# First norm of a decoder layer: rounded copies on GpSimd, scaling on ScalarE alone, projections started behind four tiles

## What is computed

```python
def rmsnorm(x, g):
    xf = x.astype(jnp.float32)
    y = xf * lax.rsqrt(jnp.mean(xf * xf, axis=-1, keepdims=True) + EPS)
    return (y * g.astype(jnp.float32)).astype(x.dtype)
...
    h = rmsnorm(x, w['norm1_g'])
    proj = h @ w['w_in']
...
    x = x + merged @ w['w_out']
    h2 = rmsnorm(x, w['norm2_g'])
    up = h2 @ w['ffn_up']
    x = x + (jax.nn.silu(g_ff) * u_ff) @ w['ffn_down']
```

## Time and profile before

| what | value |
|---|---|
| median of 3 runs | 1821.24 us |
| lowest, highest | 1820.85, 1821.57 us |
| the profiled execution, its own time | 1820.36 us |
| its span in the profile | 1818.4 us |
| PE busy | 1759.6 us (97% of the span) |
| DVE busy | 1047.0 us (58%) |
| POOL busy | 771.4 us (42%) |
| ACT busy | 518.5 us (29%) |

### The profile page before, as it was taken

The page is one execution under the profiler, slowest core; times in us unless marked ns, Lnnn a source line. Parts: engine busy times, 40 slices in busy tenths (PEclk is TensorE's granted clock), DMA queues, the critical chain, the costliest instruction groups (busy, mean ns, idle before and its releaser), DMA issues.

```text
span 1818.4 us, 31230 instructions
## 1 busy us (share of the span) xinstructions
PE 1759.6 (97%) x11711; PEld 1695.9 (93%) x11711; DVE 1047.0 (58%) x1459; ACT 518.5 (29%) x730; POOL 771.4 (42%) x622
## 2 busy tenths in 40 slices
PE   6999989999999999999999999899999999999997
PEld 5999877888899989999999999899999999999997
DVE  6774356536543344232253389977677778666666
ACT  6110144423321122011031032544444444200012
POOL 2433210123223343343352234699989895323330
PEclk9999999999999999999999999999999999999999
DMA  5111220032132222322325421322222225422302
GB/s 157 37 45 41 73 68 25 13 88 70 42 90 71 83 80 71 99 62 73 88 64 132 125 83 48 94 71 70 88 75 82 70 70 213 153 95 94 114 0 96
DMA packets 168917, 146.10 MB, mean 80 GB/s; under 512 B 14679, under 2 KB 151772, under 8 KB 168791
## 3 DMA queue, kind: packets, MB, share of 16 engines
q1 hardware_dynamic: 164983, 131.72, 24.2%
q10 hardware_dynamic: 3841, 13.14, 1.9%
HBM read 111.59 MB, written 33.21 MB: 80 GB/s over the span
## 4 chain that ended last, share of the span: by engine, by line
PE 54%; DVE 9%; POOL 6%; issue 2%; ACT 1%; DMA 0%; POOLq 0%; DVEq 0%; SPq 0%; ACTq 0%
PE ps L2678 8%; PE ps L2684 8%; PE ps L2681 8%; PE ps L3159 5%; DVE cv L2481 2%; PE ps L3285 2%; PE ps L3279 2%; PE ps L3282 2%; PE ps L3309 2%; PE pt L3309 2%; PE ps L3311 2%; PE ps L3310 2%; PE pt L3311 2%; PE pt L3310 2%; POOL slot L1326 2%
## 5 line engine op out<-in xcount | busy, mean ns | idle before, releaser
L1175 POOL TENSOR_TENSOR mark<-eps 128x1 f32<-128x1 f32 x123 | 41.3, 336 | 778.5 <-PE ps L2684 283.8
L2678 PE MATMUL ps<-h_hi,w_hi 128*128 128x352 f32 x1608 | 358.7, 331 | 7.1 <-ACT y_all L1524 5.0
L2684 PE MATMUL ps<-h_hi,w_lo 128*128 128x352 f32 x1608 | 346.9, 323 | 0.0
L2681 PE MATMUL ps<-h_lo,w_hi 128*128 128x352 f32 x1608 | 346.2, 323 | 0.0
L2678 PEld LDWEIGHTS ps<-h_hi,w_hi 128*128 128x128 f32 x1608 | 267.5, 189 | 13.2 <-issue 10.7
L2684 PEld LDWEIGHTS ps<-h_hi,w_lo 128*128 128x128 f32 x1608 | 275.5, 188 | 0.0
L2681 PEld LDWEIGHTS ps<-h_lo,w_hi 128*128 128x128 f32 x1608 | 273.4, 188 | 0.0
L1182 POOL TENSOR_TENSOR w_lo<-w_raw,w_hi 128x1024 fp32r<-128x1024 f32 x69 | 181.0, 2623 | 5.5
L2481 DVE SCALAR_TENSOR_TENSOR cv<-ext,pv,cv 128x1072 f32<-128x1072 f32 x88 | 168.3, 1912 | 9.3 <-DVE fstate L2479 2.0
L2602 DVE TENSOR_TENSOR x_acc<-x_acc,ps 128x352 f32<-128x352 f32 (+3 forms) x136 | 70.4, 518 | 43.1 <-PE ps L3311 39.1
L2602 DVE TENSOR_TENSOR x_acc<-x_acc,pt 128x352 f32<-128x352 f32 (+2 forms) x128 | 67.1, 524 | 47.4 <-PE pt L3311 44.6
(11 more groups left out here) (463 smaller groups left out, 4035.6 us busy)
## 6 DMA issues: line engine op xcount, KB each, us to landing
w_raw<-in_w_in SPq DMA_DIRECT2D x52, 512.0 KB, 4.4
w_raw<-in_ffn_up SPq DMA_DIRECT2D x26, 512.0 KB, 4.3
act_in<-act_dram SPq DMA_DIRECT2D x11, 1056.0 KB, 5.3
act_dram<-cv SPq DMA_DIRECT2D x22, 512.0 KB, 2.7
y_all<-in_ffn_up SPq DMA_DIRECT2D x18, 512.0 KB, 4.7
gates_dram<-y_all ACTq DMA_DIRECT2D x16, 528.0 KB, 2.7
cst<-gates_dram SPq DMA_DIRECT2D x16, 528.0 KB, 3.6
w_raw<-in_ffn_down SPq DMA_DIRECT2D x12, 512.0 KB, 4.3
```

Source lines behind the costliest of these rows:

```text
L2678: mm(dst[:, c, 0:CH], f_hi[n][:, k, :], h_hi[:, k, tok], start=k == 0, stop=False)
L2681: mm(dst[:, c, 0:CH], f_hi[n][:, k, :], h_lo[:, k, tok], start=False, stop=False)
L2684: last = mm(dst[:, c, 0:CH], f_lo[n][:, k, :], h_hi[:, k, tok], start=False, stop=k == KD - 1)
```

## The change

The rounded copies of step 7 move from ACT to GpSimd: `h_upper(0)` between the splits of jobs 0 and 1, `h_upper(1)` to `h_upper(8)` behind them. Step 4 is one ACT instruction of 1024 columns; the DVE instruction L1956 goes, and with it the semaphore `x_half`. The order of DVE becomes, per turn i: `inverse` i+1, `h_full` i, `h_lower` i-1. TensorE starts chunk (0,0) behind four turns in place of five, and turns 4 to 8 stand inside the chunks: 4 and 5 in chunk (0,0) ahead of steps 3 and 7, 6 in (1,0) ahead of step 5, 7 and 8 in (0,1) ahead of steps 2 and 7.

```diff
         def load_x(i):
             if i >= 3:
                 sp.wait_ge(x_normed, i - 2)
-                sp.wait_ge(x_half, i - 2)
...
+        def h_upper(i):
+
+            r = rows_of(i)
+            for half in range(2):
+                pt_drained(gp, ("x", i, half))
+            od.run(g.tensor_copy(h_hi[:, :, i * P:i * P + r], h_f[i % 2][:, :, 0:r]), h_hi_done)
+
         split_job(0)
+        h_upper(0)
         split_job(1)
+        for i in range(1, NT + 1):
+            h_upper(i)
...
-            od.run(sc.activation(x_scaled[i % 2][0:r, 0:D // 2], x_tok[i % 3][0:r, 0:D // 2], ACT.Copy,
-                                 scale=stat[0:r, 2, i:i + 1]), x_half)
+            od.run(sc.activation(x_scaled[i % 2][0:r, :], x_tok[i % 3][0:r, :], ACT.Copy,
+                                 scale=stat[0:r, 2, i:i + 1]), x_normed)
             if i < NT:
                 root_mean_square(i + 1)
-            if i >= 1:
-                h_hi_copy(i - 1)
-        h_hi_copy(NT)
...
         inverse(0)
+        pt_filled(dve, ("gain",))
+        od.run(v.tensor_copy(pv[:, 0:8], pt_of(("gain",))[:, 0:8]), ptf_of(("gain",)))
         for i in range(NT + 1):
-            r = rows_of(i)
-            od.run(v.tensor_scalar(x_scaled[i % 2][0:r, D // 2:D], x_tok[i % 3][0:r, D // 2:D], stat[0:r, 2, i:i + 1],
-                                   None, ALU.mult), x_normed)
-            if i == 0:
-                pt_filled(dve, ("gain",))
-                od.run(v.tensor_copy(pv[:, 0:8], pt_of(("gain",))[:, 0:8]), ptf_of(("gain",)))
-            if i >= 1:
-                h_full(i - 1)
             if i < NT:
                 inverse(i + 1)
-            if i >= 2:
-                h_lower(i - 2)
-        h_full(NT)
-        h_lower(NT - 1)
+            h_full(i)
+            if i >= 1:
+                h_lower(i - 1)
         h_lower(NT)
...
-                pe.wait_ge((x_half, x_normed)[half], i + 1)
+                if half == 0:
+                    pe.wait_ge(x_normed, i + 1)
...
             for k in range(KD):
+                for i in (between or {}).get(k, ()):
+                    turn_x(i)
                 mm(dst, w_hi[n][:, k, :], h_hi[:, k, tok], start=k == 0, stop=False)
...
-        chunk_after = {4: (0, 0), 5: (1, 0), 7: (0, 1), 8: (1, 1)}
-        for i in range(NT + 1):
+        for i in range(4):
             turn_x(i)
-            if i in chunk_after:
-                project_chunk(*chunk_after[i])
+        project_chunk(0, 0, {3: [4], 7: [5]})
+        project_chunk(1, 0, {5: [6]})
+        project_chunk(0, 1, {2: [7], 7: [8]})
+        project_chunk(1, 1)
```

More of the change, by code:

```diff
@@ L458, in decoder_layer @@
     pool_own, act_own, dve_own = sem("pool_own"), sem("act_own"), sem("dve_own")
-    x_inv, x_half = sem("x_inv"), sem("x_half")
-    x_sq, x_normed, h_hi_done, h_split = sem("x_sq"), sem("x_normed"), sem("h_hi_done"), sem("h_split")
+    x_inv, x_normed = sem("x_inv"), sem("x_normed")
+    x_sq, h_hi_done, h_split = sem("x_sq"), sem("h_hi_done"), sem("h_split")
     slot_full = [sem(f"slot_full{n}") for n in range(2)]
@@ L1406, in _ @@
         act.dma_start(vec3[:, :], fw[88:132, :]).then_inc(ld_vec, 16)
-        def h_hi_copy(i):
-            r = rows_of(i)
-            for half in range(2):
-                pt_drained(act, ("x", i, half))
-            od.run(sc.activation(h_hi[:, :, i * P:i * P + r], h_f[i % 2][:, :, 0:r], ACT.Copy), h_hi_done)
         def root_mean_square(i):
@@ L2725, in turn_x, with project_chunk @@
                 last.then_inc(pt_full, 1)
-        def project_chunk(n, c):
+        def project_chunk(n, c, between=None):
             s = JOBS[n][:2]
```

## The result

| | before | after |
|---|---|---|
| median of the executions (20 each, side by side) | 1820.78 us | 1825.71 us |
| lowest to highest | 1818.76 to 1824.80 | 1821.20 to 1828.16 |
| after over before, 95% interval | | 1.0022 (1.0015 to 1.0028) |
| profiled execution, own time (its span) | 1820.36 (1818.4) | 1822.54 (1820.8) |

The kernel became 4.9 us slower by the medians and 4.0 us by the ratio (interval 2.7 to 5.1), just over what can be told from no change, and lies 1.3 us above the range. The profiled execution is among the quick ones of its kernel: it shows 2.4 us of the difference in span. So there are two questions: what happened ahead of 57.5 us, and what the rest is.

What follows compares the result with a forecast made beforehand. VectorE's pace in the norm was taken to bound TensorE until about 25 us, then TensorE's own work; -0.1 (early clock rise) or +0.7 us (late) gave a middle of +0.3, median 1821.5 us, range 1819.6 to 1824.4.

Steps and rivals of the forecast that it cites:

- c = 1.05: GpSimd's rounded copy of 1024 columns, written as eight pieces of 128: forecast to take 1.05 us each.
- Copies 1 and 2 behind the split until 20.8: GpSimd in the norm: two copies after job 1's split ends at 18.6 us, finishing at 19.7 and 20.8 us.
- Copy 2 wins against remainder 1: Norm, tile 1: GpSimd's copy starts before VectorE's remainder, which then ends at 21.9 us; TensorE starts chunk (0,0) at 24.9.
- rival (b): Norm: GpSimd comes first in every tile, slowing VectorE's pace to 3.8 us; +3.0 on the sum, 1824.5 us; chance 0.12.
- rival (c): Norm: GpSimd's strided copy is slow, leaving the noise from 1.8 us per copy, at most 1827.4 us; chance 0.06.
- (a): Norm: the shared port is not in the way, chunk (0,0) starts at 23.1 to 24.0; 1819.6 to 1820.6 us; chance 0.27.
- 17.24 + 0.8: From chunk (0,1)'s start to the last matmul of (1,2): 17.24 us as before, plus 0.8 for turn 7, now inside.
- The late end: TensorE's clock rises late in the norm, chunk (0,1) starts at 38.7 us, and the end of (1,2) moves +0.7 us.
- the middle: End of chunk (1,2): +0.3 us, taken between -0.1 for an early clock rise and +0.7 for a late one.
- behind it everything follows in the same order and with the same waits: Behind 57.5 us, where `project(2)` starts: no order or wait changes, so a shift there reaches the end one for one.
- again behind the wait at 37: Sign of a wrong forecast: TensorE at its lower clock again after its wait ahead of chunk (0,1); no size given.
- any new wait behind 60 us: Sign of a wrong forecast: a wait after the norm stage that the kernel before lacks; no size given.

Runs made afterwards that it cites:

- the padding: Changed kernel plus nine one-column copies on ScalarE behind its loop of the norm, replacing the instructions moved to GpSimd: 1822.8 us, ratio 1.0008 to the kernel before.

## Why the prediction was wrong

**The stage of the norm was right, step by step.** Copy c = 1.05: 1.04. Copies 1 and 2 behind the split until 20.8: until 20.98 (the 17.6 of the sum for the end of the second split is 17.7 by its own terms, which changes nothing). Copy 2 wins against remainder 1: it did (2.07 us), and chunk (0,0) started at 25.11 for 24.9. DVE wins in the steady state, so rival (b) did not come; rival (c) neither, at c = 1.04; and nothing of (a), since at tile 1 the copy came first. The collision that the page "GPSIMD Engine Reference" of the Trainium skill speaks of in section 1, "Specifications", is in the rows above in both directions: whoever comes second takes 0.8 to 1.0 us longer.

**A term of the sum was taken from the wrong end.** The rise of the clock came late, at 29.7 us, so chunk (0,1) started at 38.84 (38.7 was the number for that end). The rest took 56.92 - 38.84 = 18.08 us from there for 17.24 + 0.8. The late end gave + 0.7 us and the trace shows + 0.88; the sum had taken the middle, + 0.3. Over several traces it is + 1.1. This term is 0.6 to 0.8 us too small. The Trainium skill ("TensorE: Matmul & The Clock Gate", part 1) says that the same kernel starts with another number of slow matmuls from run to run. The traces agree: the rise came at 29.65 and 29.96 us in two executions of the changed kernel, and at 28.03, 28.98, 29.76 and 30.92 in four kernels with the same norm and order. So I had no ground for a middle between two ends either.

**The step that failed** is "behind it everything follows in the same order and with the same waits, so a shift there should arrive at the end one for one". The order is the same. But a wait at 494 us was not: ScalarE, nine instructions shorter, answered TensorE 0.27 us later. And a shift does not arrive one for one, since nearly every execution loses 1.5 us here and there to falls of the clock. The longer wait was followed by one in 4 of 9 traces (2 of 7, where it was 0.3 us longer, and 2 of 2, where it was 0.5), the shorter or filled one in none of 11. By the estimate above the clock costs the changed kernel 2.7 us more than the one before, the largest part of the difference. Taking the longer wait away, by a fill or by the padding, took 2.0 to 3.9 us off; why the place at 494 us is worth that much stays open. The prediction named the lower rate "again behind the wait at 37" and "any new wait behind 60 us" as what would prove it wrong, and gave neither a price. A new wait did come, at 213 us, in one of the changed kernel's two executions, and lasted 1.24 us there. The earlier trace rows had shown the price at 240 us: three matmuls in 1.22 us behind 2.73 us of waiting. I read it for the rise in the norm alone and did not ask what it cost there, or how many such places the kernel has.

The chance of 0.07 for slower by over 0.2% came from rival (c) and part of (b), mechanisms of the norm. None of it was for what did come.

## What to carry to other kernels

Where TensorE is busy 97% of the span, look through the whole trace for its waits of about a microsecond and more and at the granted clock behind each: they can cost more than they last. A change to one engine's instruction stream can lengthen such a wait hundreds of microseconds later; compare the waits of both kernels over the whole span before you believe that a stage is all that moved. And do not take useful work out of TensorE's idle time at the lower clock: turn 4 was free there, and the order without it cost 1.5 us, with the clock rising later.

## What the runs showed of the hardware

- Nine transposes of no use, in a wait that TensorE had anyway, took 3.3 to 3.9 us off a kernel of 1825 us. The same fill in the kernel before, whose wait was 0.29 us shorter, took nothing.
- Nine idle instructions on ScalarE at 40 to 44 us made a table load at 493 us answer TensorE 0.27 us sooner. By what means the place in the stream decides it, no run here shows.
- In a wait of 3.0 to 3.2 us at 1290 us, the same in all 20 profiled executions, the clock fell in nine of them, for 3.4 or 6.8 us.
- The clock also fell in or behind stretches in which TensorE was busy without a break, but with small operands (behind 44 transposes of 16 rows at 983 us, and in the spatial mix at 141 to 149 us, with its matmuls of 4 rows and of 64 columns), in 7 and in 11 of the 20 profiled executions.
- A remainder on VectorE and a copy on GpSimd hold each other up, first come first served: 1.22 and 2.00 us when the remainder starts 0.1 us ahead, 2.07 and 1.04 when the copy does.
